# Own homes for the split operands of the second block's four feed-forward parts (one core, Trainium2)

## What is computed

```python
def swiglu(x, wi, wo):
    gate, up = jnp.split(x @ wi, 2, axis=-1)     # wi: 1024 x 5632
    return (jax.nn.silu(gate) * up) @ wo         # wo: 2816 x 1024
...
    for i in range(DEPTH):
        h = h + 0.5 * rms_norm_2(swiglu(rms_norm_2(h, g[0]), ffn_wi[i, 0], ffn_wo[i, 0]), g[1])
        ...
        h = h + 0.5 * rms_norm_2(swiglu(rms_norm_2(h, g[4]), ffn_wi[i, 1], ffn_wo[i, 1]), g[5])
```

## Time and profile before

| what | value |
|---|---|
| median of three runs | 2618.41 us |
| the profiled execution, span from first to last instruction | 2618.2 us |
| TensorE busy | 2498.0 us, 95% |
| VectorE, ScalarE, GpSimd busy | 61%, 51%, 22% |
| mean granted TensorE clock | 0.985 |
| DMA, mean over the span | 172 GB/s |
| four `up` stages, four `down` stages of the second block | about 126 us and 59.8 us each |

### The profile page before, as it was taken

One profiled execution on the slowest core, in us unless ns is written; L12 is line 12 of the kernel. 1 busy time (PEld: TensorE's weight loads), 2 busy tenths in 40 slices (PEclk: granted clock), 3 DMA queues, 4 the chain that ended last, 5 costly groups with the idle time before them and its releaser, 6 DMA issues. The chain is left out here.

```text
span 2618.2 us, 46369 instructions
## 1 busy us (share of the span) xinstructions
PE 2498.0 (95%) x17358; PEld 2204.9 (84%) x17358; DVE 1609.7 (61%) x2387; ACT 1333.9 (51%) x2155; POOL 585.6 (22%) x429
## 2 busy tenths in 40 slices
PE   6999999999899998999999999997999999989998
PEld 5876899888599988876899899886998899758986
DVE  3654777566477757774777466545665654556545
ACT  3434566454547644535477454444554554455544
POOL 1110333221022321101233232020231232112311
PEclk9999999999999999999999999998999999989999
DMA  8565555556245655464455566562466466524663
GB/s 282 179 227 192 153 177 185 166 184 197 77 136 173 186 164 159 151 223 160 153 178 184 192 203 197 161 210 76 130 193 194 153 196 191 170 80 141 188 200 122
DMA packets 332945, 450.54 MB, mean 172 GB/s; under 512 B 28192, under 2 KB 207392, under 8 KB 332768
## 3 DMA queue, kind: packets, MB, share of 16 engines
q1 hardware_dynamic: 332400, 446.58, 54.2%
q0 software_dynamic: 368, 1.57, 0.2%
HBM read 446.99 MB, written 1.05 MB: 171 GB/s over the span
## 5 line engine op out<-in xcount | busy, mean ns | idle before, releaser
L744 DVE TENSOR_TENSOR wlo<-raw,whi 128x1024 fp32r<-128x1024 f32 (+4 forms) x631 | 806.6, 1291 | 657.8 <-ACT whi L738 652.6
L738 ACT CAST whi<-raw 128x1024 fp32r<-128x1024 f32 (+2 forms) x776 | 768.3, 1006 | 664.5 <-PE S L1041 238.3
L1057 PE MATMUL S<-hhi,whi 128*128 128x256 f32 x1952 | 546.6, 280 | 4.0 <-DVE wlo L744 2.5
L1057 PE MATMUL S<-hlo,whi 128*128 128x256 f32 x1952 | 544.4, 279 | 1.2 <-DVE hlo L1966 1.1
L1057 PE MATMUL S<-hhi,wlo 128*128 128x256 f32 x1952 | 544.5, 279 | 0.0
L744 POOL TENSOR_TENSOR wlo<-raw,whi 128x1024 fp32r<-128x1024 f32 (+3 forms) x145 | 338.4, 2334 | 708.6 <-ACT whi L738 707.6
L1057 PEld LDWEIGHTS S<-hhi,whi 128*128 128x128 f32 x1952 | 366.4, 188 | 5.6 <-issue 4.0
L1057 PEld LDWEIGHTS S<-hlo,whi 128*128 128x128 f32 x1952 | 366.5, 188 | 1.8 <-DVE hlo L1966 1.7
L1057 PEld LDWEIGHTS S<-hhi,wlo 128*128 128x128 f32 x1952 | 366.4, 188 | 0.0
L1057 PE MATMUL G<-hhi,whi 128*128 128x256 f32 x1088 | 305.4, 281 | 0.7 <-ACT hhi L1412 0.4
L1057 PE MATMUL G<-hlo,whi 128*128 128x256 f32 x1088 | 302.2, 280 | 0.1
(11 more groups left out here) (372 smaller groups left out, 4450.6 us busy)
## 6 DMA issues: line engine op xcount, KB each, us to landing
raw<-in_ffn_wi SPq DMA_DIRECT2D x352, 256.0 KB, 3.5
raw<-in_w_up SPq DMA_DIRECT2D x264, 256.0 KB, 3.5
modw<-in_w_mod SPq DMA_DIRECT2D x192, 256.0 KB, 4.8
raw<-in_w_in SPq DMA_DIRECT2D x192, 256.0 KB, 3.0
raw<-in_ffn_wo SPq DMA_DIRECT2D x160, 256.0 KB, 3.5
raw<-in_w_down SPq DMA_DIRECT2D x120, 256.0 KB, 3.3
raw<-in_a_wqkv SPq DMA_DIRECT2D x72, 256.0 KB, 3.0
raw<-in_w_o SPq DMA_DIRECT2D x48, 256.0 KB, 3.2
```

The lines of the kernel that those rows point to most:

```text
L738: act.copy(whi[:, n0 % SPLIT, z, w], raw[:, n0 % RAW, z, w]).then_inc(hi_done, 1)
L744: eng.tensor_tensor(wlo[:, n0 % SPLIT, z, w], raw[:, n0 % RAW, z, w], whi[:, n0 % SPLIT, z, w].bitcast(F32), ALU.subtract)\
L1057: mm = pe.matmul(out_[:, m * T:(m + 1) * T], w, x, start=first and c == 0 and m == 0 and z == 0, stop=last and c == kc - 1 and z == len(te ...
```

## The change

Each part gets its own offsets for the four operands. Nothing is added to or taken from any engine's work, and no wait is changed; the functions `hidden` and `by_rows` pick the tensor of a part when the program is built.

```diff
+WIDE_HOMES = ((4, 4), (8, 8), (32, 12), (48, 0))
+DOWN_HOMES = (4, 8, 64, 192)
...
-        ybuf, hlo, rlo, probT0 = region(KD * T + SHIFT, [("ybuf", SHIFT, [P, NT, D], F32), ("hlo", SHIFT, [P, KD, T], F32R),
...
+            + [(f"wide{z}_lo", lo, [P, KD, T], F32R) for z, (_, lo) in enumerate(WIDE_HOMES)])
...
+            + [(f"wide{z}_hi", hi, [P, KD, T], F32R) for z, (hi, _) in enumerate(WIDE_HOMES)])
...
-             ("b2_fhi", 0, [P, NF, T], F32R),
-             ("b2_flo", NF * T, [P, NF, T], F32R)])
+             *[(f"b2_f{name}{z}", home + part * NF * T, [P, NF, T], F32R)
+               for z, home in enumerate(DOWN_HOMES) for part, name in enumerate(("hi", "lo"))]])
...
+        def hidden(st):
+
+            z = [z for z in STAGES[:STAGES.index(st) + 1] if z.kind == "up" and not z.conv][-1]
+            return down_parts[2 * wides.index(z):2 * wides.index(z) + 2]
...
-            return (hhi, hlo) if st.wide else (rhi, rlo)
+            if st.wide:
+                z = wide_norms.index(st)
+                return wide_hi[z], wide_lo[z]
+            return rhi, rlo
...
-                    product(st, hhi, hlo, True)
+                    product(st, *((hhi, hlo) if st.conv else by_rows(STAGES[STAGES.index(st) - 1])), True)
...
-                    product(st, *((fThi1, fTlo1) if st.conv else (fThi2, fTlo2)), False)
+                    product(st, *((fThi1, fTlo1) if st.conv else hidden(st)), False)
...
-                            act.copy(fThi2[:, at(k * 2 + b), :].rearrange("p a t -> p (a t)"), fprod[:, b, :]).then_inc(fhi_done, 1)
+                            act.copy(hidden(st)[0][:, at(k * 2 + b), :].rearrange("p a t -> p (a t)"), fprod[:, b, :]).then_inc(fhi_done, 1)
```

More of the change, by code:

```diff
@@ L413, in build @@
             ("junk", 6 * T, [P, 2, T], F32)])
-        ybuf, hlo, rlo, probT0 = region(KD * T + SHIFT, [("ybuf", SHIFT, [P, NT, D], F32), ("hlo", SHIFT, [P, KD, T], F32R),
-                                                         ("rlo", 0, [P, KD, T], F32R), ("probT0", 0, [P, KD, T], F32)])
-        hhi, rhi, probT1 = region(KD * T + LINES - SHIFT, [("hhi", 0, [P, KD, T], F32R), ("rhi", LINES - SHIFT, [P, KD, T], F32R),
-                                                   ("probT1", 0, [P, KD, T], F32)])
+        ybuf, hlo, rlo, probT0, *wide_lo = region(
+            KD * T + SHIFT, [("ybuf", SHIFT, [P, NT, D], F32), ("hlo", SHIFT, [P, KD, T], F32R),
+                             ("rlo", 0, [P, KD, T], F32R), ("probT0", 0, [P, KD, T], F32)]
+            + [(f"wide{z}_lo", lo, [P, KD, T], F32R) for z, (_, lo) in enumerate(WIDE_HOMES)])
+        hhi, rhi, probT1, *wide_hi = region(
+            KD * T + LINES - SHIFT, [("hhi", 0, [P, KD, T], F32R), ("rhi", LINES - SHIFT, [P, KD, T], F32R),
+                                     ("probT1", 0, [P, KD, T], F32)]
+            + [(f"wide{z}_hi", hi, [P, KD, T], F32R) for z, (hi, _) in enumerate(WIDE_HOMES)])
         probT = [probT0, probT1]
@@ L433, in build @@
         (qkv1, qT1, qgT, gT, kT1, kgT, v1, vg, oThi1, oTlo1, fThi1, fTlo1,
-         qkvA, qkvB, kdupB, sgate, sgained, qT2, kT2, sm, mask, order, pT, phi, plo, oThi2, oTlo2, fThi2, fTlo2) = region(max(n1, n2), [
+         qkvA, qkvB, kdupB, sgate, sgained, qT2, kT2, sm, mask, order, pT, phi, plo, oThi2, oTlo2, *down_parts) = region(max(n1, n2), [
              ("b1_qkv", 0, [P, NT, C_GATE], F32),
@@ L574, in build @@
         wides = [st for st in STAGES if st.kind == "up" and not st.conv]
+        wide_norms = [st for st in STAGES if st.kind == "norm2" and st.wide]
+        def hidden(st):
+            z = [z for z in STAGES[:STAGES.index(st) + 1] if z.kind == "up" and not z.conv][-1]
+            return down_parts[2 * wides.index(z):2 * wides.index(z) + 2]
         def inner(st):
@@ L2328, in chunks_lo @@
                     def chunks_lo(k, j, i):
-                        flo = fTlo1 if st.conv else fTlo2
-                        fhi = fThi1 if st.conv else fThi2
+                        fhi, flo = (fThi1, fTlo1) if st.conv else hidden(st)
                         for b in range(2):
```

## The result

The changed kernel takes 2625.66 us (median of 11 runs, 2620.20 to 2627.51), the kernel before, measured beside it, 2617.89 us (11 runs, 2612.72 to 2620.92): 1.0030 times as long, with a 95% interval from 1.0022 to 1.0038. It is slower by 0.3%, 7.8 us; the interval is 5.8 to 9.9 us.

What follows compares the result with a forecast made beforehand. It took TensorE to be the bound, through the start-to-start distance of matmuls in eight stages. Terms 2.3 + 0.8 + 0 + 1.7 + 0 = +4.8 us on 2618.4 gave 2623.2 us, range 2606 to 2638 us.

Steps and rivals of the forecast that it cites:

- What is full: Eight `up` and `down` stages: TensorE busy 2498.0 of 2618.2 us; the change acts only on the distance between matmul starts.
- Part 3's `up`: Both operands go to d = 0: 120.0 ns per matmul, +2.3 us, bounds -4.7 and +7.0 us.
- Parts 0 and 1's `up`: `lo` at 32 costs 1.1 ns on 352 matmuls, `hi` at 96 nothing: +0.4 us a part, +0.8 us.
- Parts 0 and 1's `down`: d = 224, taken as halfway between 0 and 192: 3.3 ns for 264 matmuls, +1.7 us, bounds 0 and +3.5 us.
- Part 2's `up`: 704 matmuls go to d = 192; one row for gain, one for loss: 0, between -3.1 and +4.6 us.
- Parts 2 and 3's `down`, the period, the 32-byte steps: `down`s 256 and 768 bytes further keep d = 0, cost 0; period read as 256 bytes; allocator steps 32 bytes.
- The writes: Operand chunks written by ScalarE, VectorE and GpSimd (475, 476, 744 ns) at new homes: taken as 0.
- Rival 1: All eight stages: homes do nothing, something else sets the rhythm; 2618.4 us; chance 0.18.
- Rival 3: Parts 0 and 1: 32-byte-off moving operand costs 6.6 ns per `up` matmul, `up`s 124 ns or more; 2638.1 us; chance 0.17.
- Rival 2: `up`s: new homes let in the 113.4 ns rhythm; 2609.1 us for two `up`s, 2599.7 for all four; chance 0.20.

Runs made afterwards that it cites:

- the map: Six single-execution runs on the changed kernel, `up` operands moved to free room, homes varied by part: `up` 113.4 to 122.1 ns, `down` 226.7 to 234.3 ns.
- the two halves: Changed kernel with only the `down`s' new homes, 2619.61 us (ratio 1.0009 to the kernel before), and with only the `up`s', 2621.89 us (1.0018).
- the fourth map: Map kernel with `up`s' hi and lo at (16, 0), (0, 16), both 240, both 12; `down`s 176, 248, 252, 512 bytes on; first two `up`s 118.4, 118.6 ns.
- the third map: Map kernel with `up`s at d = 8, 24, 48, 112, `down`s 240, 208, 8, 4 bytes on; `up` at 112 took 113.4 ns.
- the sixth: Map kernel with `up`s at d = 144, 176, 208, 368, `down`s 144, 80, 112, 236 bytes on; `up` at 368 took 113.4 ns.
- the last two kernels: Map's kernel with all four `up`s at d = 112, `down`s at 0: 2596.62 us; kernel before with first block's products at d = 112 too: 2584.35 us.

## Why the prediction held

The forecast was 2623.2 us, a little slower; measured were 2625.66 us and +7.8 us for the forecast's +4.8, which lies under the measured interval of 5.8 to 9.9 us. The way and the place were right; two of its three costs were taken at less than half, 2.5 us for 6.0 us, and the total stayed close because both are small. By its steps:

- **What is full.** Right: TensorE's distance is the time of these stages, and nothing else moved with the homes. The writes and TensorE's waits at the start of part 0's `up` (1.1 and 0.4 us) are as before.
- **Part 3's `up`.** The surplus at d = 0 carried from 384 and 512 columns to 256 gave 120.0 ns and +2.3 us; measured 120.00 ns and +2.3 us. The best step, made from two groups of rows and no theory, and partly luck: in the map, d = 0 is the only difference with the same surplus in both columns (13.3 ns over the columns' time); at d = 112 it is 6.7 ns in the `up` and 13.3 in the `down`, at d = 96 13.3 and 20.0.
- **Parts 0 and 1's `up`.** Mis-sized: +0.8 us forecast for both, +2.5 us measured (118.95 ns). The step gave 1.1 ns to the `lo` third and nothing to the rest. The run with unlike homes shows `hi` at 96 alone at 118.0 ns and `lo` at 32 alone at 117.8 ns, each for the whole stage, so most of the 1.17 ns belongs to neither but to their sequence, and a sum over terms could not have found it.
- **Parts 0 and 1's `down`.** Mis-sized: +1.7 us forecast, +3.5 us measured. The step took a home halfway between two known ones to cost half; the map shows that a value between two points means nothing here. The upper bound, the worst row of that form at hand, was met exactly.
- **Part 2's `up`.** Right at 0 (117.81 ns), between a row for gain and a row for loss. Neither row said much: the same 256 columns of `in` that took 113.3 ns took 117.8 ns in the first such stage of that trace (last section), and in other traces the 384 columns take 173.3 ns.
- **Parts 2 and 3's `down`, the period, the 32-byte steps.** Right: 226.7 ns at 256 and 768, and parts 0 and 1 are alike to 0.01 ns.
- **The writes.** Right at 0, as their durations and the two halves show.

Rival 1 (homes do nothing) is out: the same `down` takes 59.8 or 61.5 us. The Trainium skill (SBUF — State Buffer, "Who interferes with whom") says that TensorE never waits on anyone. The traces agree in that the stretches compared here hold no wait on another engine; but TensorE's distance depends on where its own two operands stand, which that rule leaves no room for. Rival 3 is out: a start 16 bytes off (116.7 ns) is better than the old home, and no home tried reached its 124 ns. Rival 2 named the right thing that was not in this change: the 113.4 ns rhythm can be had by a home, d = 112. The Trainium skill's start-to-start time (an estimate of 109.2 ns for 256 columns from TensorE: Matmul & The Clock Gate, "Wait — 56ns, not 53.3ns?") isn't reached by any home tried; the best is 113.3 ns.

## What to carry to other kernels

Where TensorE reloads its weights for every matmul and has no waits, read the distance from start to start, not the recorded duration, and compare the same form with operands in different places: here it was worth 113 to 122 ns. Within one form of product the difference between the two operands' addresses modulo 256 bytes sets it, but for a second distance at some homes; give each operand of a product the same difference, and measure it for each form rather than interpolate or carry it over, since 4 bytes can cost 8 ns. One kernel with a different home in each of several equal stages gives a point per stage from a single profile.

## What was not expected

**One home can have two rhythms.** At d = 64 a stage, or a unit of 96 matmuls, runs at 117.8 ns or at 113.3 ns. In the 13 traces with this home the one never turns into the other while each matmul starts within 126 ns of the last; the change comes only where some start late. The stages that no experiment changed show it: the `gates` at about 1062 us, same instructions and homes, first in the run with the `down`s alone, then by its windows in the changed kernel above:

```profile
1061.70:1095.70 34.00, 33.97 (x288) 33.98 (x288) 1.00 0.44 138
```

34.0 us here and 32.8 there. It was at 113.3 ns in 4 of the 13 traces that have it at d = 64. A whole `up` of the first block took 120.9 us in the fourth map, all but its first 50 matmuls in the short rhythm, and 125.3 us in the kernel before:

```profile
1307.40:1428.30 120.90, 120.57 (x1055) 119.95 (x1054) 1.00 0.61 189
```

Another did so in the profile of the kernel with four `up`s at d = 112. None of the twelve `up`s of the second block that stood at d = 64 did. The 256 columns of `in`, at d = 192, have both distances too: 113.3 ns in the earlier trace rows, and 117.8 ns in the first such stage of the same trace, 36 matmuls from the first of these starts to the second:

```profile
46.63 0.28 PE L1041 MATMUL S<-whi,hhi 128*128 128x256 f32 x1
...
50.87 0.28 PE L1041 MATMUL S<-whi,hhi 128*128 128x256 f32 x1
```

So a point of the map that was seen once may have a second value.

All thirteen `up`s at d = 112 or 368 had the short one (one in the third map, one in the sixth, four and seven in the last two kernels), so the home seems to take the choice away. What decides it at d = 64 is open. It may be behind the scatter of the kernel before, 2609.44 to 2622.68 us over all its runs, since one `up` in the short rhythm is 4.7 us; no profile shows that.

**The distances are fractions of one step.** 113.33, 116.67, 117.78, 118.33, 120.00 ns are 17, 17 1/2, 17 2/3, 17 3/4 and 18 times 6.67 ns, and 226.67, 230.00 and 233.33 ns are 34, 34 1/2 and 35 times; 6.67 ns is the time of 16 columns, 64 bytes of one partition, at 2.4 GHz. The starts don't fall on that grid one by one (117, 118, 118 ns), only sums over a few matmuls do. Others need larger denominators: 118.67 ns is 17 4/5 times, 117.14 ns 17 4/7. It would fit two readers that take turns at pieces of 64 bytes; that is a guess from the numbers and wasn't tested.
